# The first weight unit of four layers on the scaled but not yet normalized activations

## The chip, the cores and the metric

The program runs on one core of one Trainium2 chip. The metric is the device time of one execution in microseconds (us). The kernel before takes 989.41 us, the median of 3 runs (989.23 to 990.48).

## What is computed

Batch 1, 256 tokens, width 1024, all of it in fp32. Five residual layers follow each other: EVEN and ODD (the first block), then F1, MIX and F2 (the second block: FFN, mixer, FFN). Each opens with an RMS norm and a modulation whose shift and scale come from a conditioning vector, and closes with a gated residual update:

```python
def rms_norm(x, gain):
    y = x * lax.rsqrt(jnp.mean(x * x, axis=-1, keepdims=True) + EPS)
    return y * gain

def modulate(h, shift, scale):
    return h * (1 + scale[:, None, :]) + shift[:, None, :]
...
    h = modulate(rms_norm(x, ffn1_norm[l]), sh1, sc1)
    x = x + 0.5 * g1[:, None, :] * swiglu(h, ffn1_w_gate[l], ffn1_w_up[l], ffn1_w_down[l])
    h = modulate(rms_norm(x, mix_norm[l]), sh2, sc2)
    proj = h @ w_in[l]
...
def swiglu(h, w_gate, w_up, w_down):
    return (jax.nn.silu(h @ w_gate) * (h @ w_up)) @ w_down
```

Between ODD and F1 the first block's final norm is applied too, so two roots are needed there. Shifts, scales and gates are the columns of `cond @ W` with W of 1024 by 24576 in all; these weights are read like all the others.

## The kernel before

**Layout.** x and h are kept transposed: 8 tiles of 128 channels by 256 tokens. `xT` is the residual, `SQT` a work tile, `hh` and `hl` the high and low part of h (fp32 is split into two fp32r numbers, and a product is three matmuls: high by high, high by low, low by high). Weights come in units of 1 MB, each in two halves ("pieces") of 128x1024, from DRAM into `ring` (10 slots, filled in program order by SyncE), then ScalarE writes the high part into `WH` (4 slots, `cut`) and VectorE the low part into `WL` (4 slots, `cut`); both run two or three pieces ahead of TensorE, and a slot is free when TensorE has used its piece. `unit_list` writes the order of the units by hand, and `weave` strews the units of the modulation weights ("ada") between those of a layer; they are multiplied on VectorE (two instructions of 128x1024 per unit, L1676 or L1673), in `ada_places` behind the piece of the unit that follows.

**A unit.** `cols_T` is a unit of 256 output columns: for each of the 8 tiles of h 6 matmuls, 128 weight columns stationary and 256 tokens moving. `wide` (FFN gate and up, and others) has 128 tokens stationary and 512 weight columns moving. `out_rows` is a unit of the layer's output projection, which sums into `pacc` over all of a layer's units.

**Where two layers meet.** The last output unit (`finish`) gives `pacc` in four quarters of two tiles. VectorE adds each quarter to `xT` (`update`, L1770), ScalarE squares it (`squares`), TensorE sums the squares over the channels (64 small matmuls with ones, `stats`). VectorE takes the reciprocal root of two numbers per partition (`rsqrt`, 9 small instructions, L1710 to L1727), TensorE spreads it over the partitions (`spread`, bank `r`), and for each of the 8 tiles VectorE computes SQT = x times scale times root (L1756), ScalarE hh = SQT plus shift, VectorE hl = SQT plus shift minus hh (L1761). Only then does TensorE start on the first unit of the layer: `qk0` (ODD), `f1g0`, `wu0` (MIX), `f2g0`. Warm-up matmuls (`warm`) stand in the gap.

In the MIX layer `wu0` and `wu1` give the input of a state space part. ScalarE (12 copies per unit) and VectorE (4) rearrange it into `UR` (`urs`), and `s5_in(0)` and `s5_in(1)` on TensorE read it. `s5_in(0)` stands right behind `wu1`. In the FFN layers each block is a gate and an up unit and, one block later, a down unit; before it, the product is turned by four transposes (`turn`, L1022).

## Time and profile before

| | |
|---|---|
| median of 3 runs | 989.41 us |
| the profiled execution's own time | 992.07 us |
| its span in the trace | 990.3 us |
| PE busy | 954.0 us (96%) |
| weight loads busy | 876.7 us (89%) |
| VectorE (DVE) busy | 714.2 us (72%) |
| ScalarE (ACT) busy | 507.6 us (51%) |
| read from DRAM | 217.25 MB, 220 GB/s over the span |

The table is of the whole span. All queries and the hand-made schedules below are made on the one profiled execution, whose own time is 2.66 us above the median. A busy PE is not a PE at its peak, since matmuls overlap in the trace: work is told from waiting by the distance from one start to the next.

### The profile page before, as it was taken

To read this page: it belongs to the slowest core of one execution; us is meant where nothing else is said; L and a number is where in the kernel's file an instruction comes from. 1 tells how busy PE (TensorE), PEld (TensorE's weight loads), DVE (VectorE), ACT (ScalarE), POOL (GpSimd) and SP (SyncE) were. 2 spreads that over 40 slices of the span, in tenths; PEclk is the share of its full clock that TensorE was granted. 3 is DMA by queue.
4 is the path that set the end of the run, shared out by engine and by line. 5 is a ranking of instruction groups with operands and counts; after the bars stand their busy time and mean duration, and the time that the engine had idled before them with its cause. 6 is when DMAs were issued, how large, how long until landed. Compare 5 with 4: busy or idle time off the path is not lost.

```text
span 990.3 us, 17238 instructions
## 1 busy us (share of the span) xinstructions
PE 954.0 (96%) x7025; PEld 876.7 (89%) x7025; DVE 714.2 (72%) x994; ACT 507.6 (51%) x745; POOL 41.8 (4%) x68
## 2 busy tenths in 40 slices
PE   6999999999999999999999999999999999999998
PEld 6799999989799789999778888889998978898987
DVE  4778877767866766576899988977988765465554
ACT  4654364456544446544755456474646454444444
POOL 2100000000000003320100000000000000000000
PEclk9999999999999999999999999999999999999999
DMA  9987586844875894658378887776534457474731
GB/s 363 384 279 257 184 290 234 297 167 150 273 248 183 287 302 153 234 214 300 84 242 270 292 276 251 265 251 216 153 124 126 153 170 234 149 262 143 253 110 43
DMA packets 134247, 219.43 MB, mean 222 GB/s; under 512 B 8585, under 2 KB 100090, under 8 KB 134168
## 3 DMA queue, kind: packets, MB, share of 16 engines
q1 hardware_dynamic: 132416, 214.99, 64.9%
q0 software_dynamic: 992, 1.76, 0.7%
q10 hardware_dynamic: 760, 1.59, 0.4%
q8 instruction: 55, 0.90, 0.4%
q14 instruction: 24, 0.20, 0.1%
HBM read 217.25 MB, written 1.05 MB: 220 GB/s over the span
## 4 chain that ended last, share of the span: by engine, by line
PE 75%; DVE 11%; DMA 6%; issue 4%; ACT 4%; SPq 0%; ACTq 0%; DVEq 0%
PE pw L569 50%; PE pacc L569 24%; DMA ring<-in_odd_in_w 3%; DVE ACC L1676 3%; DVE WL L1660 2%; ACT WH L1175 1%; ACT AR L1175 1%; DMA ring<-in_ada_w 1%; DVE SQT L1756 1%; DVE hl L1761 1%; PE pw L1022 1%; DMA ring<-in_odd_out_w 1%; DMA ring<-in_ffn_w_down 1%; ACT hh L1175 1%; DMA cst<-in_consts 1%
## 5 line engine op out<-in xcount | busy, mean ns | idle before, releaser
L1175 ACT ACTIVATE WH<-ring 128x1024 fp32r<-128x1024 f32 x288 | 302.6, 1057 | 300.1 <-PE pw L569 125.0
L1660 DVE TENSOR_TENSOR WL<-ring,WH 128x1024 fp32r<-128x1024 f32 x288 | 348.0, 1224 | 90.8 <-ACT WH L1175 90.1
L569 PE MATMUL pacc<-YH,WH 128*128 128x256 f32 x672 | 192.9, 287 | 2.6 <-issue 1.7
L569 PE MATMUL pw<-hh,WH 128*128 128x256 f32 x704 | 187.8, 288 | 4.4 <-ACT AR L1175 2.1
L569 PE MATMUL pacc<-YH,WL 128*128 128x256 f32 x672 | 190.1, 283 | 0.0
L569 PE MATMUL pacc<-YL,WH 128*128 128x256 f32 x672 | 190.1, 283 | 0.0
L569 PE MATMUL pw<-hh,WL 128*128 128x256 f32 x704 | 184.9, 284 | 0.0
L569 PE MATMUL pw<-WH,hh 128*128 128x512 f32 x448 | 177.0, 395 | 4.4 <-DVE WL L1660 4.0
L569 PE MATMUL pw<-WL,hh 128*128 128x512 f32 x448 | 174.9, 390 | 0.0
L569 PEld LDWEIGHTS pw<-hh,WH 128*128 128x128 f32 x704 | 135.7, 193 | 9.2 <-issue 6.3
L569 PE MATMUL pw<-hl,WH 128*128 128x256 f32 x704 | 142.7, 284 | 0.0
L569 PE MATMUL pw<-WH,hl 128*128 128x512 f32 x448 | 138.1, 389 | 0.0
L569 PEld LDWEIGHTS pw<-hh,WL 128*128 128x128 f32 x704 | 135.8, 193 | 0.1
L569 PEld LDWEIGHTS pacc<-YH,WH 128*128 128x128 f32 x672 | 128.8, 192 | 5.9 <-issue 3.9
L569 PEld LDWEIGHTS pacc<-YL,WH 128*128 128x128 f32 x672 | 128.9, 192 | 0.7
L569 PEld LDWEIGHTS pacc<-YH,WL 128*128 128x128 f32 x672 | 128.8, 192 | 0.0
L1175 ACT ACTIVATE AR<-pw 128x512 f32<-128x512 f32 (+8 forms) x180 | 80.1, 466 | 94.3 <-PE pw L569 93.4
L1676 DVE SCALAR_TENSOR_TENSOR ACC<-ring,PC,ACC 128x1024 f32<-128x1024 f32 x95 | 121.7, 1281 | 2.9 <-DMA ring<-in_ada_w 2.7
L569 PEld LDWEIGHTS pw<-hl,WH 128*128 128x128 f32 x704 | 110.3, 193 | 0.1
L569 PEld LDWEIGHTS pw<-WH,hh 128*128 128x128 f32 x448 | 84.2, 188 | 25.1 <-DVE WL L1660 6.9
L569 PEld LDWEIGHTS pw<-WH,hl 128*128 128x128 f32 x448 | 84.1, 188 | 18.0
L569 PEld LDWEIGHTS pw<-WL,hh 128*128 128x128 f32 x448 | 84.2, 188 | 16.3
(272 smaller groups left out, 782.2 us busy)
## 6 DMA issues: line engine op xcount, KB each, us to landing
ring<-in_w_mod SPq DMA_DIRECT2D x72, 512.0 KB, 5.6
ring<-in_odd_in_w SPq DMA_DIRECT2D x56, 512.0 KB, 6.0
ring<-in_ada_w SPq DMA_DIRECT2D x48, 512.0 KB, 6.8
ring<-in_ffn_w_gate SPq DMA_DIRECT2D x88, 256.0 KB, 3.6
ring<-in_ffn_w_up SPq DMA_DIRECT2D x88, 256.0 KB, 4.5
ring<-in_ffn_w_down SPq DMA_DIRECT2D x44, 512.0 KB, 5.1
ring<-in_even_in_w SPq DMA_DIRECT2D x40, 512.0 KB, 7.4
ring<-in_even_out_w SPq DMA_DIRECT2D x16, 512.0 KB, 6.4
```

Of the source, the lines that this page charges most:

```text
L569: return eng.matmul(o, a, b, start=start, stop=stop, skip_group_check=True)
L1022: last = eng.transpose(pb[:, n * T + m * P:n * T + m * P + P], fbuf(blk, m)[:, n * P:n * P + P], ident)
L1175: return eng.activation(dst, src, func, **kw)
L1660: tt(WL[:, i % NL, :], slot(half_of(i)), WH[:, i % NH, :].bitcast(F32), SUB).then_inc(s_lo, 1)
L1676: stt(out=acc, in0=slot(g), scalar=wc, in1=acc, op0=MUL, op1=ADD).then_inc(s_ada, 1)
L1756: stt(out=SQT[:, k, :], in0=xT[:, k, :], scalar=GS[:, k:k + 1], in1=rb, op0=MUL, op1=MUL).then_inc(s_u, 1)
L1761: stt(out=hl[:, q, :], in0=SQT[:, q, :], scalar=m[:, q:q + 1], in1=hh[:, q, :].bitcast(F32), op0=ADD, op1=SUB).then_inc(s_hl, 1)
```

## The change

**What it does.** For ODD, F1, MIX and F2 the first unit no longer waits for the root. The product W(x·scale·root + shift) is written as root·W(x·scale) + W·shift: the root depends on the token alone and the shift on the channel alone.

- ScalarE writes x·scale into hh as soon as a quarter of x is updated (`early`), VectorE the low part (`early_lows`). hh and hl are two columns wider and hold the shift there, so one matmul of 258 moving columns does both products (`first`).
- Half of the sums of squares come after the first two tiles of that unit, the spreading of the root after the fifth.
- The other units read the fully modulated h, as before. It is now made while the first unit runs; h takes the place of x·scale.
- When the first unit is read, VectorE multiplies it by the root (`unnormed`, after all of `modulate`), then ScalarE adds the shift's product as a bias: into GQ (ODD), within the Silu (F1, F2), or into a new tile UT (MIX), from which `urs` now copies.
- The first FFN block's gate and up units are of the `cols_T` kind (96 matmuls of 256 columns in place of 48 of 512), and its four transposes are gone.
- The ada units leave the last 5 and, but for EVEN, the first 3 units of each layer. 20 of them now stand in 28 of ODD's 36 units (33 before), 16 in 25 of F1's 33 (30 before). QUIET names units at which no modulation work is done.
- All `warm` at these four places are gone. A table load of ScalarE's moves ahead of the squares (ODD), another into the units before (F1). GpSimd's four loads for F1's side work are issued after unit oo1, not oo7. Side work in F1 starts four pieces later.

```diff
@@ unit_list @@
-    def weave(side, from_, clear=0):
+    def weave(side, from_, clear=0, lead=0):
...
-            while k < len(side) and (2 * k + 1) * (len(main) - clear) <= 2 * i * len(side):
+            while k < len(side) and (2 * k + 1) * (len(main) - clear - lead) <= 2 * (i - lead) * len(side):
...
     def ffn(tag, Wg, Wu, Wd):
         for b in range(12):
-            if b < 11:
+            if b == 0:
+                cols(f"{tag}g0", Wg, 0)
+                cols(f"{tag}u0", Wu, 0)
+            elif b < 11:
...
-    weave(ada(a0, 2, 3) + ada(a1, 0, 2), at, 3)
+    weave(ada(a0, 2, 3) + ada(a1, 0, 2), at, 5)
...
-    weave(ada(a1, 2, 3) + ada(a2, 0, 4), at, 3)
+    weave(ada(a1, 2, 3) + ada(a2, 0, 4), at, 5, 3)
...
-    weave(ada(a2, 4, 8), at, 3)
+    weave(ada(a2, 4, 8), at, 5, 3)
...
-    weave(ada(a2, 8, 9), at)
+    weave(ada(a2, 8, 9), at, 5, 3)
...
+FIRST = [None, "qk0", "f1g0", "wu0", "f2g0"]
+QUIET = ("eo7", "qk0", "qk1", "oo7", "f1g0", "f1u0", "f1d10", "wu0", "wu1", "wo3", "f2g0", "f2u0", "f2d10")
@@ build @@
-        hh = sb("hh", [P, 8, T], F32R)
-        hl = sb("hl", [P, 8, T], F32R)
+        hh = sb("hh", [P, 8, T + 2], F32R)
+        hl = sb("hl", [P, 8, T + 2], F32R)
...
         def urs(copy, j, quadrants):
-            pb = v3(pw[place[f"wu{j}"]][:, :], 2).rearrange("p m (c s) -> p m c s", s=4)
+            src = UT if j == 0 else v3(pw[place["wu1"]][:, :], 2)
+            pb = src.rearrange("p m (c s) -> p m c s", s=4)
@@ TensorE @@
-            def norm_mod(L, z):
-                ada("tail " + TAIL[L - 1])
-                back(f"fin{L - 1}")
-                if L >= L_MIX:
-                    warm(5, f"warm{L}a")
-                spread(f"r{L}", 0, z, (s_u, 8 * L + 8), True)
-                warm(4, f"warm{L}b")
+            def first(L, z, c=0):
+                name = FIRST[L]
+                k, a = unit(name)
+                names = early_names(L)
+                bks = [open_(nm, None, True) for nm in names]
+                for half in range(2):
+                    H, Lo = piece(2 * k + half, a)
+                    for kk in range(4):
+                        i = 4 * half + kk
+                        if i == 2:
+                            later[L - 1]()
+                            back(f"fin{L - 1}")
+                        if i == 5:
+                            spread(f"r{L}", c, z, (s_rb, L), True)
+                        p.wait_ge(s_eh, 8 * (L - 1) + i + 1)
+                        for m, pb in enumerate(bks):
+                            mm(pb[:, 0:T + 2], H[:, kk, m * P:m * P + P], hh[:, i, :], i == 0, False)
+                            mm(pb[:, 0:T + 2], Lo[:, kk, m * P:m * P + P], hh[:, i, :], False, False)
+                        p.wait_ge(s_el, 8 * (L - 1) + i + 1)
+                        for m, pb in enumerate(bks):
+                            last = mm(pb[:, 0:T + 2], H[:, kk, m * P:m * P + P], hl[:, i, :], False, i == 7)
+                    last.then_inc(s_use, 1)
...
-            for j in range(2):
-                cols_T(L_MIX, f"wu{j}", [(s_ura, j + 1), (s_urd, j + 1)])
+            first(L_MIX, 5)
+            cols_T(L_MIX, "wu1", [(s_ura, 2), (s_urd, 2)])
             s5_in(0)
@@ ScalarE @@
+            def early(L, sh, c):
+                s.wait_ge(s_gs, L + 1)
+                s.wait_ge(*gone[f"ada{c}"])
+                s.wait_ge(*used(LAST_H[L]))
+                act(hh[:, :, T:T + 2], shift_cols(sh)).then_inc(s_esh, 1)
+                for q in range(4):
+                    ns = (2 * q, 2 * q + 1)
+                    if q == 3:
+                        cut_on(L - 1)
+                        squares(L - 1, ns)
+                    for n in ns:
+                        s.wait_ge(s_x, X_FIN[L - 1] + n + 1)
+                        act(hh[:, n, 0:T], xT[:, n, :], scale=GS[:, n:n + 1]).then_inc(s_eh, 1)
+                    if q < 3:
+                        squares(L - 1, ns)
+                k = unit(FIRST[L])
+                cut(2 * k)
+                modulate(L, sh, range(4))
+                cut(2 * k + 1)
+                modulate(L, sh, range(4, 8))
+                act(RB[L], pw[place[f"r{L}"]][:, 0:T]).then_inc(s_rb, 1)
+
+            def offsets(L, scale=1.0):
+                for m, nm in enumerate(early_names(L)):
+                    s.wait_ge(*full[nm])
+                    act(ES[:, m:m + 1], pw[place[nm]][:, T:T + 1], scale=scale).then_inc(s_es, 1)
...
-            for nm in ("wu0", "wu1", "wc0", "wv0"):
+            offsets(L_MIX)
+            for m, nm in enumerate(early_names(L_MIX)):
+                s.wait_ge(*gone[nm])
+                act(UT[:, m, :], UT[:, m, :], ACT.Identity, bias=ES[:, m:m + 1]).then_inc(s_ut, 1)
+            s.wait_ge(s_ut, 2)
+            urs(act, 0, (0, 1, 2)).then_inc(s_ura, 1)
+            for nm in ("wu1", "wc0", "wv0"):
                 win(nm)
@@ VectorE @@
+            def between(L, g, sh, root):
+                v.wait_ge(s_esh, L)
+                tt(hl[:, :, T:T + 2], shift_cols(sh), hh[:, :, T:T + 2].bitcast(F32), SUB)
+                update(L - 1, g, lambda q: early_lows(L, (2 * q - 2, 2 * q - 1)))
+                k = unit(FIRST[L])
+                cut(2 * k)
+                root()
+                early_lows(L, (6, 7))
+                mods[0] += 1
+                modulate(L, sh, range(4))
+                cut(2 * k + 1)
+                modulate(L, sh, range(4, 8))
+
+            def unnormed(L, dsts):
+                v.wait_ge(s_rb, L)
+                for m, nm in enumerate(early_names(L)):
+                    v.wait_ge(s_es, 2 * (L - 1) + m + 1)
+                    tt(dsts[m], RB[L], pw[place[nm]][:, 0:T], MUL).then_inc(s_bank[place[nm]], 1)
@@ GpSimd @@
-            g.wait_ge(*used("oo7"))
+            g.wait_ge(*used("oo1"))
```

**How instructions move.** On VectorE, where MIX hands over to F2 (`xT` is the update, `hl` the low part, `WL` a weight piece's low part, `RS` the root). Before, from the last weight pieces of MIX:

```order
L1660 TENSOR_TENSOR WL<-ring,WH 128x1024 x6
L1770 SCALAR_TENSOR_TENSOR xT<-pacc,MOD,xT 128x256 x8
L1745 SCALAR_TENSOR_TENSOR PC<-MOD,VC 128x8
L1710 TENSOR_SCALAR RS<-pw 128x2
L1720 TENSOR_SCALAR RS<-RS 128x2
```

Now:

```order
L1728 TENSOR_TENSOR WL<-ring,WH 128x1024 x6
L1813 SCALAR_TENSOR_TENSOR PC<-MOD,VC 128x8
L1845 TENSOR_TENSOR hl<-MOD,hh 128x8x2
L1868 SCALAR_TENSOR_TENSOR xT<-pacc,MOD,xT 128x256 x4
L1825 SCALAR_TENSOR_TENSOR hl<-xT,PC,hh 128x256 x2
L1868 SCALAR_TENSOR_TENSOR xT<-pacc,MOD,xT 128x256 x2
L1825 SCALAR_TENSOR_TENSOR hl<-xT,PC,hh 128x256 x2
L1868 SCALAR_TENSOR_TENSOR xT<-pacc,MOD,xT 128x256 x2
L1825 SCALAR_TENSOR_TENSOR hl<-xT,PC,hh 128x256 x2
L1728 TENSOR_TENSOR WL<-ring,WH 128x1024
L1778 TENSOR_SCALAR RS<-pw 128x2
L1788 TENSOR_SCALAR RS<-RS 128x2
```

The eight updates are taken apart by six of the low parts, and a weight piece stands ahead of the root.

The same engine at the end of this hand-over, from the last products x·scale·root (`SQT`) on. Before:

```order
L1756 SCALAR_TENSOR_TENSOR SQT<-xT,PC,pw 128x256
L1761 SCALAR_TENSOR_TENSOR hl<-SQT,MOD,hh 128x256
L1756 SCALAR_TENSOR_TENSOR SQT<-xT,PC,pw 128x256
L1761 SCALAR_TENSOR_TENSOR hl<-SQT,MOD,hh 128x256 x2
L1660 TENSOR_TENSOR WL<-ring,WH 128x1024 x4
L2192 TENSOR_TENSOR AR<-AR,pw 128x256 x2
```

Now:

```order
L1838 SCALAR_TENSOR_TENSOR hl<-SQT,MOD,hh 128x256
L1833 SCALAR_TENSOR_TENSOR SQT<-xT,PC,pw 128x256
L1838 SCALAR_TENSOR_TENSOR hl<-SQT,MOD,hh 128x256
L1833 SCALAR_TENSOR_TENSOR SQT<-xT,PC,pw 128x256
L1838 SCALAR_TENSOR_TENSOR hl<-SQT,MOD,hh 128x256 x2
L1860 TENSOR_TENSOR AR<-AR,pw 128x256 x2
L1728 TENSOR_TENSOR WL<-ring,WH 128x1024 x2
L2287 TENSOR_TENSOR AR<-AR,pw 128x256 x2
```

The first weight piece behind the hand-over stands behind two products more, `AR<-AR,pw`, which are the first unit times the root.

On ScalarE, where F1 hands over to MIX. Before, from the squares to the copies into UR of the first unit:

```order
L1175 ACTIVATE SQT<-xT 128x256 x8
L1175 ACTIVATE WH<-ring 128x1024
L1175 ACTIVATE hh<-SQT,MOD 128x256 x8
L1175 ACTIVATE WH<-ring 128x1024 x2
L1175 ACTIVATE AR<-pw 32x2x64 x12
```

Now, from the last two high parts of x·scale on:

```order
L1205 ACTIVATE hh<-xT,PC 128x256 x2
L1205 ACTIVATE WH<-ring 128x1024
L1205 ACTIVATE hh<-SQT,MOD 128x256 x4
L1205 ACTIVATE WH<-ring 128x1024
L1205 ACTIVATE hh<-SQT,MOD 128x256 x4
L1205 ACTIVATE AR<-pw 128x256
L1205 ACTIVATE RS<-pw 128x1 x2
L1205 ACTIVATE AR<-AR,RS 128x256 x2
L1205 ACTIVATE AR<-AR 32x2x64 x12
```

The 12 copies of `wu0` stood two pieces behind the eight high parts of h. They now stand behind a copy of the root's bank, two columns of the shift's product and two biases.

## Rows read from the trace of the kernel before

**Rows 1.** The page: busy time by engine, and the chain that ended last.
```profile
PE 954.0 (96%) x7025; PEld 876.7 (89%) x7025; DVE 714.2 (72%) x994; ACT 507.6 (51%) x745; POOL 41.8 (4%) x68
...
PE 75%; DVE 11%; DMA 6%; issue 4%; ACT 4%; SPq 0%; ACTq 0%; DVEq 0%
```

**Rows 2.** Timeline, PE, 784 to 809 us: start us, duration us, instruction, [idle before].
```profile
784.82 2.09 PE L569 MATMUL pw<-cst,SQT 128*64 128x64 f32 x64
...
788.78 0.68 PE L569 MATMUL pw<-cst,RS 128*128 128x128 f32 x4 [0.56 <-DVE RS L1727]
...
790.67 0.47 PE L569 MATMUL pw<-WH,hh 128*128 128x512 f32 x1 [0.31 <-ACT hh L1175]
...
797.63 0.50 PE L569 MATMUL pw<-WH,hh 128*128 128x512 f32 x1 [1.27 <-DVE WL L1660]
...
803.23 0.39 PE L569 MATMUL pw<-WH,hh 128*128 128x512 f32 x1
...
808.67 0.60 PE L1022 MATMUL pw<-cst,AR 128*128 128x128 f32 x4
```

**Rows 3.** Timeline, DVE, 781 to 801 us.
```profile
781.48 1.65 DVE L1770 SCALAR_TENSOR_TENSOR xT<-pacc,MOD,xT 128x256 f32<-128x256 f32 x4
...
787.03 0.16 DVE L1710 TENSOR_SCALAR RS<-pw 128x2 f32<-128x2 f32 x1 [1.02 <-PE pw L569]
...
789.50 0.87 DVE L1756 SCALAR_TENSOR_TENSOR SQT<-xT,PC,pw 128x256 f32<-128x256 f32 x2 [0.87 <-PE pw L569]
...
795.96 0.48 DVE L1761 SCALAR_TENSOR_TENSOR hl<-SQT,MOD,hh 128x256 fp32r<-128x256 f32 x1 [0.18 <-ACT hh L1175]
...
796.36 4.63 DVE L1660 TENSOR_TENSOR WL<-ring,WH 128x1024 fp32r<-128x1024 f32 x4
```

**Rows 4.** Timeline, ACT, 781 to 788 us.
```profile
781.99 1.59 ACT L1175 ACTIVATE SQT<-xT 128x256 f32<-128x256 f32 x4 [1.76 <-DVE xT L1770]
...
786.16 1.04 ACT L1175 ACTIVATE WH<-ring 128x1024 fp32r<-128x1024 f32 x1
```

**Rows 5.** Timeline, PE, the places to which the other three layers are followed.
```profile
222.65 0.28 PE L569 MATMUL pw<-hh,GRH 128*16 128x256 f32 x1
...
231.22 1.13 PE L569 MATMUL pw<-AR 16*128 16x256 f32 x8
...
492.79 0.39 PE L569 MATMUL pw<-WH,hh 128*128 128x512 f32 x1
...
701.35 3.68 PE L569 MATMUL pw<-AR 128*128 128x64 f32 x32
```

**Rows 6.** Timeline, DVE, last instruction ahead of each of these layers' updates.
```profile
205.21 1.22 DVE L1660 TENSOR_TENSOR WL<-ring,WH 128x1024 fp32r<-128x1024 f32 x1 [1.66 <-ACT WH L1175]
...
467.28 1.23 DVE L1660 TENSOR_TENSOR WL<-ring,WH 128x1024 fp32r<-128x1024 f32 x1 [1.65 <-ACT WH L1175]
...
678.44 0.17 DVE L2200 TENSOR_SCALAR PC<-MOD 128x8 f32<-128x8 f32 x1
```

**Rows 7.** Timeline, ACT, a table load and the copies to UR.
```profile
220.89 1.28 ACT L1316 ACT_TABLE_LOAD   x1
...
695.46 3.32 ACT L1175 ACTIVATE AR<-pw 32x128 f32<-32x128 f32 x12
```

**Rows 8.** Stretches: us, busy us of engines (instructions), PEclk, DMA share, GB/s.
```profile
210.00:214.00 4.00, 2.13 (x65) 2.02 (x62) 2.12 (x12) 1.75 (x3) 0.00 (x0) 1.00 0.02 6
...
214.00:218.00 4.00, 3.76 (x23) 3.50 (x22) 3.36 (x9) 1.92 (x4) 0.00 (x0) 0.62 0.01 4
...
320.00:326.00 6.00, 3.86 (x35) 2.91 (x34) 5.84 (x11) 1.64 (x3) 0.00 (x0) 1.00 0.95 334
```

**Rows 9.** A stretch of the F1 layer, columns as in rows 8.
```profile
490.00:670.00 180.00, 177.97 (x1097) 154.57 (x1096) 158.89 (x206) 102.07 (x152) 0.23 (x2) 1.00 0.78 259
```

**Rows 10.** Timeline, DVE and PE, 258 us: a half of a modulation unit, and a stall.
```profile
258.72 1.28 DVE L1676 SCALAR_TENSOR_TENSOR ACC<-ring,PC,ACC 128x1024 f32<-128x1024 f32 x1
...
258.85 0.50 PE L569 MATMUL pw<-WH,hh 128*128 128x512 f32 x1 [0.40 <-DVE WL L1660]
```

More of the change, by code:

```diff
@@ L223, in ada_places @@
                 held += [m - 2, m - 1]
-        else:
+        elif nm not in quiet:
             add(nm)
@@ L2182, in ffn @@
             def ffn(tag, y0, n0):
-                for blk in range(12):
+                pieces(f"{tag}u0")
+                if tag == "f1":
+                    side.rate = 1
+                b = place[f"{tag}u0"]
+                for m in range(2):
+                    v.wait_ge(*full[f"{tag}u0"])
+                    v.wait_ge(s_sl, n0 + m + 1)
+                    a = tt(fbuf(0, m), fbuf(0, m), pw[b][:, m * T:m * T + T], MUL)
+                a.then_inc(s_bank[b], 1)
+                for blk in range(1, 12):
                     if blk < 11:
@@ L2336, in _, with first_rows @@
             side.rate = 4
-            win("wu0")
-            win("wu1")
+            def first_rows():
+                v.wait_ge(s_ut, 2)
+                urs(copy, 0, (3,)).then_inc(s_urd, 1)
+            pieces("wu1", first_rows)
+            v.wait_ge(*full["wu1"])
+            urs(copy, 1, (3,)).then_inc(s_urd, 1)
             side.gens.append(s5_states(0))
```

232 lines of the change are left out of this document (120 added, 112 removed).

## The prediction

> **What bounds the kernel.** I read the page first. TensorE (PE) is busy for 96% of the span and holds 75% of the chain that ended last; VectorE (DVE) is next with 11% [rows 1]. So only time in which PE waits can be won, and of PE's own work the change removes next to none. Then I went through the timelines of the four places where a layer hands over to the next, MIX to F2 in full. PE has its last sums of squares from 784.82 to 786.9, spreads the root at 788.78, starts the first unit at 790.67 and waits once more at 797.63 for a weight piece's low part; the second FFN block starts at 803.23 [rows 2]. The last product starts 0.1 ahead of the sums, so 18.5 us pass until then for 13.0 us of work (2.1 of sums and 10.9 of the unit pair, 48 matmuls by 0.227, which is 5.44 for 24 from 803.23 to 808.67). 5.5 us are lost. The other three places lose about as much, so some 22 us of 990 lie here: the most that the change could aim at.
>
> What holds PE there is VectorE. From the root on it takes 0.395 us per instruction of 256 columns, two for each tile: 6.94 us from the first product (789.50) to the next weight piece (796.36, with 0.08 of overlap taken back) [rows 3]. PE needs 0.72 per tile (6 matmuls by 0.121). The question is what becomes of VectorE's chain when PE's wait goes.
>
> **VectorE's chain after the change, with MIX to F2 as the model.** I call x0 the start of the first update. A weight piece was at 780.34 to 781.57 and x0 at 781.48 [rows 3] (0.1 of overlap). Now the scale's columns, ScalarE's copy of the shift and its low part come first, three small instructions handed between engines, 0.2 each as in the root's steps: x0 = 782.15. From there:
>
> - Updates, squares and high parts. ScalarE now has four instructions per pair of tiles where it had two. Four take 1.59 [rows 4], the same as VectorE's two updates and two low parts. Three pairs need 0.5 + 3 x 1.6 = 5.3, then ScalarE puts a weight piece (1.04 [rows 4]) ahead of the last squares. VectorE's own piece waits for it and starts at x0 + 6.45.
> - That piece: 1.16 until the next instruction (4 in 4.63 [rows 3]): 7.6. The root: 1.75 from 787.03 to 788.78, the handing over to PE in it [rows 2, 3], 1.65 without: 9.3. Two low parts: 10.15.
> - The eight tiles of modulation: 6.94, plus the piece between their halves (1.16), plus 0.55, since high part and low part start anew: 18.8.
> - The two products of the first unit by the root: 0.8, then the next weight piece, 1.2: 20.85 in all.
>
> So the second block can start at 782.15 + 20.85 = 803.0, against 803.23. PE keeps up: from 784.7 on it has 2.1 of sums, 5.8 of the first unit and 0.5 of the spread, and it waits 1.1 for ScalarE (the last squares end at x0 + 7.1, 789.25; PE would be there at 788.1): the first unit ends at 794.3; the second unit ends 0.25 behind the last low part, at 801.2. There it waits again. The wait moved from ahead of the first unit to behind the second. The four transposes that go give 0.35 more [rows 2]. **F2: 0.6 us won.**
>
> **F1.** The last piece ahead is at 467.28 [rows 6], so it ends at 468.5. One small instruction more makes x0 = 469.4, four roots in place of two add 0.25: 490.5 against 492.79 [rows 5], and 0.35 from the transposes. **2.65 won.** It is more than in F2, since from x0 to the old mark are 23.4 us here and 21.1 there.
>
> **ODD.** The piece at 205.21 [rows 6] ends at 206.4, ScalarE's table load (1.28 [rows 7]) fits beside it: x0 = 207.15. The last low part ends at 226.0. The next matmuls, those with GRH, need a bank that the first product frees at 226.5, and take 2.75 (from 222.65 to 231.22 it was these and a unit of 5.8 [rows 5]). Two units and they end at 229.3; before at 231.1. **1.85 won.** The table load cost nothing where it was; here it has 0.1 us to spare.
>
> **MIX.** HG is at 678.44 [rows 6], x0 = 679.35, the last low part ends at 698.15. Both products are done at 699.05, the biases at 699.65. Then come the 12 copies into UR, 3.32 [rows 7], which lay under `wu1` before: 703.0. `s5_in(0)` stands right behind `wu1` on PE and began at 701.35 [rows 5]. **1.65 lost.** Queued behind it are `wc0` and all of the layer, and a PE that is 96% busy [rows 1] has little slack to take it up. PE stands still from 698.4 to 703.0, 4.6 us. After about 1.9 idle us in 210 to 214 the granted clock was 0.62 over the next 4 us, so 3 us at 1.2 GHz; in 320 to 326 2.1 idle us left it at 1.00 [rows 8]. Twice that should bring it down. It falls while PE still waits, so of the 1.5 us that 3 us at half clock can cost (bounds 0 and 1.5) I take 0.9. The Trainium skill ("TensorE: Matmul & The Clock Gate", section "Why this matters for your kernels") says the same: gaps between bursts of matmuls bring the lower clock back.
>
> The copies now read SBUF instead of PSUM; I priced them as before. The Trainium skill ("VectorE: DVE Perf Modes", section on the TRN2 errata) speaks against the change here: ScalarE pays 224 cycles per instruction from SBUF and 172 from PSUM. At 1.2 GHz that is an estimate of 0.04 us for each of 12, 0.5 us later; the sum would be a loss of 2.15 in place of 1.65. No row shows these copies from SBUF.
>
> **Edits at nothing.** 258 columns: a matmul of 256 takes 0.121 and one of 512 0.227, so 256 columns cost PE 0.114 at most and two more 0.001 each, 0.2 us over 192 matmuls, beside waits. 96 matmuls of 256 for 48 of 512: 11.6 for 10.9, hidden as long as VectorE sets the end; 0.7 twice if it doesn't. The warm-ups stood in the gap. GpSimd's early loads and the later side work of F1 meet no wait on PE.
>
> **Modulation units closer together.** In ODD six halves fall on `gv0` to `gv3` where four did, and there PE already waits for low parts (0.40 at 258.85, with a half of 1.28 just ahead [rows 10]); in F1 four halves leave the opening for a stretch in which VectorE is busy for 159 of 180 us [rows 9]. Bounds: nothing, or all six at 1.2, 7.2 us. A gain is possible too: the openings are free of halves, so VectorE may catch up. I take 0.6, near the low end, since VectorE has 21 idle us in F1.
>
> **Sum.** -1.85 - 2.65 - 0.6 + 1.65 + 0.9 + 0.6 = -1.95. On the profiled execution 992.07 becomes 990.1. It stands 2.66 above the median of 989.41; I take the difference over to the median: **987.5 us**. A measurement of this kernel tells about 0.2% (2 us) from no change, so below 987.4 is faster and above 991.4 slower. The forecast lies on that edge.
>
> **Rivals.**
> - *VectorE catches up* (0.25). The openings lose eight modulation halves, 4 in F1 and 4 in ODD before `gv0`, 1.2 us each of VectorE's time, 9.6 in all. If 0.4 of that stood in PE's way, as stalls like that of rows 10, 3.8 are won on top and the 0.6 isn't paid: 983.1. For it speaks that I let VectorE's backlog set three of four ends; against it, that the weights' ring is filled in order and a half held up holds the weights behind it.
> - *Modulation work becomes the bound* (0.2), the other side. Place: `gv0` to `gv3` and F1's middle. VectorE there has 2.3 us of pieces per unit, now 1.5 us of halves, and side work. It decides as soon as a weight piece's low part comes later than PE's 2.7 us per piece. Full price: the 6.6 us that I left out, 994.1; half of it 990.8; I expect 992 to 994.
> - *The hand-overs close* (0.05): VectorE's chain runs ahead and PE never waits. Four times 3.3 (790.67 less 786.9, less 0.5 for the spread): 976. Against it stands the chain above.
> - *The first unit doesn't start early*, as a wait of `early` or of a bank holds it. Then all four places get longer by 0.8 to 2 us; I count it with the slower case.
>
> **Chances.** Forecast 0.5: its own spread is 985.5 to 990, of which 0.2 is faster, 0.28 within 0.2% and 0.02 slower. Catching up gives 0.23 faster and 0.02 same; modulation 0.05 same and 0.15 slower; closing 0.05 faster. Together 0.48, 0.35, 0.17. The range for 8 in 10 leaves out the closing case and the upper half of the slower one: 983 to 991.8.
>
> **What would show it.** In the trace after: the first unit starting within 2 us of the last product, at all four places; two waits of PE for low parts, in the second unit and behind it, 1 to 2 us each in F1 and F2; `s5_in(0)` some 4.5 us behind `wu1` with a clock under 1.00 there; a VectorE chain of 18.8 from the first update to the last low part. If that chain is shorter by over 1 us, or PE waits for ScalarE's squares for over 2 us, the model is wrong. The number is wrong with right hand-overs if `gv0` to `gv3` or F1 change by over 2 us.

## The result, and the profile after

The changed kernel takes **1014.03 us** (median of 4 runs, 1012.67 to 1016.56), the kernel before 989.89 beside it: 1.0247 times as long, 95% interval 1.0225 to 1.027. Forecast were 987.5 in a range of 983.0 to 991.8. The profiled execution took 1014.64 us, its span is 1012.9.

The page of after, the lines that answer to [rows 1]:

```profile
PE 958.6 (95%) x7047; PEld 879.7 (87%) x7047; DVE 729.4 (72%) x1038; ACT 522.7 (52%) x796; POOL 42.8 (4%) x68
...
PE 69%; DVE 12%; DMA 8%; issue 5%; ACT 5%; SPq 0%; ACTq 0%; DVEq 0%
```

PE is busy for 4.6 us more, the span is 22.6 longer. PE's share of the chain falls from 75 to 69%. VectorE, DMA, ScalarE and "issue" gained it, so most of the time went into waits and not into work, and no single engine took it.

To see where, I put the start of every unit's last matmul of both kernels side by side. Each row gives the us between two of these marks (before e1 and e17, see the experiments):

| stretch | before | after | e1 | e17 |
|---|---|---|---|---|
| start to eo7 | 209.5 | 209.7 | 209.7 | 208.4 |
| eo7 to qk3 (hand-over to ODD) | 34.3 | 31.7 | 33.5 | 31.7 |
| qk3 to gv3 | 24.7 | 23.2 | 21.7 | 23.2 |
| og0 | 9.8 | **14.2** | 10.3 | 5.9 |
| og1 to og6 | 44.1 | 44.6 | 46.3 | 51.4 |
| og7 | 9.4 | **13.7** | 12.5 | 10.7 |
| sv0 to oo6 | 134.1 | 137.0 | 136.3 | 134.8 |
| oo6 to f1g2 (hand-over to F1) | 52.7 | 46.5 | 50.3 | 47.9 |
| f1g2 to f1d10 | 163.8 | **174.7** | 169.0 | 167.7 |
| f1d10 to wc0 (hand-over to MIX) | 28.2 | **37.2** | 28.2 | 28.1 |
| wc0 to wo3 | 74.1 | 73.7 | 74.0 | 73.6 |
| wo3 to f2u1 (hand-over to F2) | 29.8 | 28.9 | 29.7 | 28.9 |
| f2u1 to f2d10 | 166.7 | 168.5 | 166.7 | 168.5 |

Three hand-overs did become shorter, by 2.6, 6.2 and 0.9 us. The largest losses lie in four other places, in bold. Among neighbouring rows the place of a loss is not firm: e14 (see the experiments) differs from the kernel before by 128 unused bytes alone, and in its profiled execution og7 takes 13.8 and sv0 to oo6 130.8. Over og7 to oo6 together the two are 144.6 and 143.5, with 150.7 in after and 148.9 in e1; that sum is the safer reading.

**The hand-over to F2 goes as drawn up.** PE and VectorE there, as in [rows 2, 3]:

```profile
809.15 1.43 PE L585 MATMUL pw<-cst,SQT 128*64 128x64 f32 x32
812.77 0.61 PE L585 MATMUL pw<-cst,RS 128*128 128x128 f32 x4
819.42 0.36 PE L585 MATMUL pw<-hh,WH 128*128 128x256 f32 x1 [1.00 <-ACT hh L1205]
823.98 0.47 PE L585 MATMUL pw<-WH,hh 128*128 128x512 f32 x1 [1.33 <-DVE WL L1728]
```
```profile
803.64 1.66 DVE L1868 SCALAR_TENSOR_TENSOR xT<-pacc,MOD,xT 128x256 f32<-128x256 f32 x4
...
821.55 0.48 DVE L1838 SCALAR_TENSOR_TENSOR hl<-SQT,MOD,hh 128x256 fp32r<-128x256 f32 x1 [0.18 <-ACT hh L1205]
821.95 0.75 DVE L1860 TENSOR_TENSOR AR<-AR,pw 128x256 f32<-128x256 f32 x2
```

The reader is to see two waits of PE, 1.00 in the second unit and 1.33 behind it, and a VectorE chain of 18.3 us from the first update (803.64) to the products behind the last low part (821.95). The forecast had two waits for low parts of 1 to 2 us and a chain of 18.8; the first of the two ends with ScalarE's high part, not with a low part. F1 shows the same pair:

```profile
493.24 0.36 PE L585 MATMUL pw<-hh,WH 128*128 128x256 f32 x1 [1.02 <-ACT hh L1205]
497.81 0.47 PE L585 MATMUL pw<-WH,hh 128*128 128x512 f32 x1 [0.85 <-DVE WL L1728]
```

**og0 and og7.** PE, then ScalarE and VectorE ahead of the second wait:

```profile
268.14 2.20 PE L585 MATMUL pw<-AR 128*128 128x128 f32 x9 [3.18 <-DVE AR L2056]
```
```profile
328.76 1.08 PE L585 MATMUL pw<-ACC,cst 128*32 128x256 f32 x8 [4.52 <-DVE ACC L1744]
```
```profile
322.70 1.06 ACT L1205 ACTIVATE WH<-ring 128x1024 fp32r<-128x1024 f32 x1 [8.88 <-DMA ring<-in_odd_in_w]
```
```profile
323.86 1.23 DVE L1728 TENSOR_TENSOR WL<-ring,WH 128x1024 fp32r<-128x1024 f32 x1 [0.65 <-ACT WH L1205]
325.00 1.28 DVE L1744 SCALAR_TENSOR_TENSOR ACC<-ring,PC,ACC 128x1024 f32<-128x1024 f32 x1
326.20 1.22 DVE L1728 TENSOR_TENSOR WL<-ring,WH 128x1024 fp32r<-128x1024 f32 x1
327.33 1.28 DVE L1744 SCALAR_TENSOR_TENSOR ACC<-ring,PC,ACC 128x1024 f32<-128x1024 f32 x1
```

At 268 PE waits for the decay's last product, which the attention matrices (`at`) need. That product, before and after:

```profile
263.38 1.22 DVE L1957 TENSOR_TENSOR AR<-AR 128x1024 f32<-128x1024 f32 x1
```
```profile
266.87 1.22 DVE L2056 TENSOR_TENSOR AR<-AR 128x1024 f32<-128x1024 f32 x1
```

It starts 3.5 us later, while PE is through with gv3 3.9 us earlier (its last matmul at 264.6, before at 268.4). So og0 gives back a lead: at its end the changed kernel is 0.5 behind. At 328 PE waits for a modulation sum, the sum for halves that stand behind weight pieces, the pieces for a transfer that ScalarE had waited 8.88 us for.

**The hand-over to MIX.** ScalarE, PE, and stretches as in [rows 8]:

```profile
711.63 0.91 ACT L1205 ACTIVATE AR<-AR,RS 128x256 f32<-128x256 f32 x2 [0.85 <-DVE AR L1860]
712.57 5.22 ACT L1205 ACTIVATE AR<-AR 32x128 f32<-32x128 f32 x12
717.81 2.00 ACT L1205 ACTIVATE WH<-ring 128x1024 fp32r<-128x1024 f32 x2
719.72 3.31 ACT L1205 ACTIVATE AR<-pw 32x128 f32<-32x128 f32 x12
```
```profile
718.04 1.30 PE L585 MATMUL pw<-AR 128*128 128x64 f32 x5 [6.53 <-ACT AR L1205]
```
```profile
711.00:715.00 4.00, 0.51 (x5) 0.31 (x3) 3.02 (x8) 3.27 (x8) 0.00 (x0) 1.00 0.17 45
...
719.00:723.00 4.00, 4.00 (x21) 4.00 (x20) 3.87 (x7) 3.87 (x13) 0.00 (x0) 0.50 0.39 129
723.00:727.00 4.00, 4.00 (x20) 4.00 (x20) 2.88 (x5) 1.10 (x2) 0.00 (x0) 0.50 0.50 137
```

The 12 copies of `wu0`, now from SBUF, take 5.22 us; the 12 of `wu1` behind them, from PSUM, take 3.31, as in [rows 7]. PE waits 6.53 us for them, until 718.04. The granted clock falls to the lower level (0.50, 1.2 GHz) at 715.5, within the wait, and stays there until 729.2: PE runs the first 11.1 us behind the wait at half clock, though it is busy all the time. From the end of wu1 to the end of wc0 pass 21.2 us where it was 9.3: 6.5 of wait, and 5.4 more, which the half clock over those 11.1 us accounts for (5.6 at most). Ahead of it 2.9 us were won, so 9.0 are left.

**F1.** PE's waits of 1 us and more between f1g2 and f1d10:

```profile
530.91 0.77 PE L1062 MATMUL pw<-cst,AR 128*128 128x128 f32 x4 [1.10 <-DVE AR L2298]
...
587.32 0.77 PE L1062 MATMUL pw<-cst,AR 128*128 128x128 f32 x4 [1.84 <-DVE AR L2298]
...
593.90 0.64 PE L585 MATMUL pw<-ACC,cst 128*32 128x256 f32 x8 [2.54 <-issue]
...
689.57 0.39 PE L585 MATMUL pacc<-YH,WH 128*128 128x256 f32 x1 [1.85 <-DVE YL L1774]
```

In before this stretch shows one wait over 0.3, of 0.44. Some 1.6 of the 10.9 us are no waits: 17 units with 512 moving columns take 5.57 in place of 5.44, and 10 others 0.06 less each (e4, which has the wider rows alone, shows 1.4 for this stretch). What VectorE does ahead of the last of these waits:

```profile
685.96 2.83 DVE L2276 TENSOR_TENSOR AR<-AR 32x512 f32<-32x512 f32 x4
688.82 0.69 DVE L1774 TENSOR_TENSOR YL<-pw,YH 128x512 fp32r<-128x512 f32 x1
```

The four instructions of 0.7 us are the last step of F1's side work (`s5_skip`). Started four pieces later, it now ends just ahead of the low part `YL` that PE's next output unit needs; in e1 it is over at 672.6, 9.7 us ahead of `YL`.

### The profile page after: what moved, and what is told of

It is laid out like the page before. It is cut to its first block, busy times and chain, and to the rows that moved or that the text cites. A ratio compares the mean times of both kernels' runs of the same rounds, so it can differ in the third digit from the quotient of the medians.

```text
span 1012.9 us, 17393 instructions
## 1 busy us (share of the span) xinstructions
PE 958.6 (95%) x7047; PEld 879.7 (87%) x7047; DVE 729.4 (72%) x1038; ACT 522.7 (52%) x796; POOL 42.8 (4%) x68
## 4 chain that ended last, share of the span: by engine, by line
PE 69%; DVE 12%; DMA 8%; issue 5%; ACT 5%; SPq 0%; ACTq 0%; DVEq 0%
PE pw L585 46%; PE pacc L585 22%; DMA ring<-in_odd_in_w 4%; DVE ACC L1744 3%; DVE WL L1728 2%; ACT AR L1205 2%; ACT WH L1205 2%; DMA ring<-in_ffn_w_up 1%; DMA ring<-in_ada_w 1%; DVE SQT L1833 1%; DVE hl L1838 1%; DMA ring<-in_even_in_w 1%; ACT hh L1205 1%; PE pw L1062 1%; DMA cst<-in_consts 1%
## 5 line engine op out<-in xcount | busy, mean ns | idle before, releaser
L585 PE MATMUL pw<-hh,WH 128*128 128x256 f32 (+1 forms) x768 | 206.2, 290 | 4.1 <-ACT hh L1205 4.0
L585 PE MATMUL pw<-hh,WL 128*128 128x256 f32 (+1 forms) x768 | 201.8, 284 | 0.0
L585 PE MATMUL pw<-WH,hh 128*128 128x512 f32 x416 | 165.6, 398 | 2.6 <-DVE WL L1728 2.6
L585 PE MATMUL pw<-WL,hh 128*128 128x512 f32 x416 | 163.9, 394 | 0.0
L585 PEld LDWEIGHTS pw<-hh,WH 128*128 128x128 f32 x768 | 146.9, 191 | 10.1 <-issue 9.3
L585 PE MATMUL pw<-hl,WH 128*128 128x256 f32 (+1 forms) x768 | 155.2, 284 | 0.0
L585 PEld LDWEIGHTS pw<-hh,WL 128*128 128x128 f32 x768 | 147.3, 192 | 0.0
L585 PE MATMUL pw<-WH,hl 128*128 128x512 f32 x416 | 130.3, 394 | 0.0
L585 PEld LDWEIGHTS pw<-hl,WH 128*128 128x128 f32 x768 | 119.3, 191 | 0.1
L585 PEld LDWEIGHTS pw<-WH,hh 128*128 128x128 f32 x416 | 78.2, 188 | 23.0 <-issue 4.8
```

What stands on the lines that cost most here:

```text
L585: return eng.matmul(o, a, b, start=start, stop=stop, skip_group_check=True)
```

## The experiments

Theories at the start: **packing**, the denser weave of the modulation alone makes weights and sums late; against it **company**, that the later decay, F1's later side work and GpSimd's earlier loads do it. For MIX **copies and clock** against a chain behind it that is just as late. For the distance of matmuls the **wider rows** of hh and hl.

**e1: the new weave in the kernel before.**

```diff
-    weave(ada(a1, 2, 3) + ada(a2, 0, 4), at, 3)
+    weave(ada(a1, 2, 3) + ada(a2, 0, 4), at, 5, 3)
...
-    weave(ada(a2, 4, 8), at, 3)
+    weave(ada(a2, 4, 8), at, 5, 3)
```

`weave` takes its last parameter as in the change.

> The kernel before, with nothing changed but the places of the modulation units of ODD and F1: 20 of them in 28 units and 16 in 25, as in the change. Theory 'packing' (the denser weave alone makes weights and the sums of the modulation late in og0 to og7 and in the middle of F1): 8 to 14 us slower than before, with most of it between gv3 and sv0 and between f1g2 and f1d10, and ScalarE waiting longer for the ring's transfers there. Rival 'company' (the other edits of the change, the later start of the decay and of F1's side work, GpSimd's earlier loads, cost it): within 2 us of before.

998.49 us, 1.0094 (1.0064 to 1.0123): 8.4 us over the kernel before beside it (990.1), for other places of the same units. The column e1 has og7 3.2 and F1's middle 5.2 longer. Its PE there:

```profile
326.06 0.99 PE L569 MATMUL pw<-ACC,cst 128*32 128x256 f32 x8 [3.81 <-DVE ACC L1676]
...
565.93 0.77 PE L1022 MATMUL pw<-cst,AR 128*128 128x128 f32 x4 [1.79 <-DVE AR L2192]
...
591.51 0.64 PE L569 MATMUL pw<-ACC,cst 128*32 128x256 f32 x8 [2.07 <-issue]
```

The same kinds of wait as in after, but not the one at the end of F1. Packing holds for 8.4 of 24.1, and og0 (10.3) is not part of it.

**e2: the changed kernel, modulation from the layer's start on.**

```diff
-    weave(ada(a1, 2, 3) + ada(a2, 0, 4), at, 5, 3)
+    weave(ada(a1, 2, 3) + ada(a2, 0, 4), at, 5)
...
-    weave(ada(a2, 4, 8), at, 5, 3)
+    weave(ada(a2, 4, 8), at, 5)
...
-QUIET = ("eo7", "qk0", "qk1", "oo7", "f1g0", "f1u0", "f1d10", "wu0", "wu1", "wo3", "f2g0", "f2u0", "f2d10")
+QUIET = ("eo7", "qk0", "oo7", "f1g0", "f1d10", "wu0", "wu1", "wo3", "f2g0", "f2u0", "f2d10")
```

> The changed kernel with the modulation units of ODD and F1 starting at the layer's first unit again (20 in 31 units and 16 in 28; the last five stay free), and with halves allowed at qk1 and f1u0. Packing: 4 to 9 us faster than the changed kernel, the hand-overs at most 1.5 us longer each. Company: within 2 us of it.

1017.9 us, 1.0287 (1.0259 to 1.0315): 3.9 slower than the changed kernel. Less dense, and no better: neither theory's number came. The loss moved: og0 to og7 took 60.2 us in place of 72.4, but qk3 to gv3 34.0 in place of 23.2. gv3 took 12.5 us and f1g3 12.9, each with a wait of 4 to 4.6 ahead of a modulation sum that stood in the unit right behind its last half. So I formed "adjacent sums" (e7).

**e3: the mixer's input read later.**

```diff
             cols_T(L_MIX, "wu1", [(s_ura, 2), (s_urd, 2)])
+            cols_T(L_MIX, "wc0")
             s5_in(0)
-            cols_T(L_MIX, "wc0")
+            cols_T(L_MIX, "wv0")
             s5_in(1)
-            cols_T(L_MIX, "wv0")
...
-            urs(act, 0, (0, 1, 2)).then_inc(s_ura, 1)
...
+            pieces("wu1")
+            urs(act, 0, (0, 1)).then_inc(s_ura, 1)
+            s.wait_ge(*full["wu1"])
+            urs(act, 1, (0, 1, 2)).then_inc(s_ura, 1)
...
-                urs(copy, 0, (3,)).then_inc(s_urd, 1)
+                urs(copy, 0, (2, 3)).then_inc(s_urd, 1)
...
-            side.gens.append(s5_states(0))
             win("wc0")
-            side.gens.append(s5_states(1))
+            side.rate = 6
+            side.gens += [s5_states(0), s5_states(1)]
```

> The changed kernel with s5_in(0) behind wc0 and s5_in(1) behind wv0 on TensorE, ScalarE's weight pieces of wu1 ahead of the copies of wu0, and 8 of the 16 copies on VectorE where it had 4. Theory 'copies and clock' (11.9 us are lost from the end of wu1 to the end of wc0, as TensorE waits 6.5 us for 12 copies from SBUF and then runs at half clock): 7 to 11 us faster than the changed kernel, no clock under 0.9 in the mixer. Rival 'chain' (the state space part behind it is as late, and TensorE waits for it at wb0 or wc1 instead): at most 3 us faster, with a wait of 4 us or more in front of s5_out(0) or s5_turn(0).

1009.71 us, 1.0197 (1.0178 to 1.0215): 4.3 faster than the changed kernel, between the two. The clock stays at 1.00 in the mixer, and f1d10 to wc0 takes 24.4 in place of 37.2, wc0 to wo3 80.2 in place of 73.7. These two can't be read apart, since `s5_in(0)`, 3.7 us of work, now stands behind wc0: together they are 104.6 in place of 110.9, 6.3 less, with 102.3 before. F1's middle takes 2.2 more. In the mixer PE now waits for VectorE's state chain, whose first part the edit also starts later:

```profile
733.65 1.09 PE L585 MATMUL pw<-AR 128*64 128x128 f32 x16 [0.76 <-DVE AR L2399]
736.61 1.09 PE L585 MATMUL pw<-AR 128*64 128x128 f32 x16 [1.87 <-DVE AR L2404]
```

**e4: the kernel before with rows of 258.** `sb("hh", [P, 8, T])` and `hl` became `T + 2` wide, every use stays 256.

> The kernel before with hh and hl two columns wider (rows of 258, of which 256 are used) and nothing else. Theory 'row pitch' (the wider rows, or the addresses that they shift, change the distance of matmuls): units with 512 moving columns take 5.57 in place of 5.44 us and those with 256 moving columns 5.69 in place of 5.76, as in the changed kernel, and the sum over the kernel is within 2 us. Rival: nothing changes, both distances stay at 227 and 120 ns.

991.48 us, 1.0016 (1.0007 to 1.0026). The wide units take 5.57, the others 5.69, as expected; the sum is small, 1.6 us.

**e5: the changed kernel, the mixer as before.**

```diff
-            early(L_MIX, M2[:, 24:32], 9)
+            squares(L_F1)
+            cut_on(L_F1)
+            modulate(L_MIX, M2[:, 24:32])
```

and its like on PE (`first(L_MIX, 5)` out, spread and warm-ups in) and VectorE.

> The changed kernel with the mixer handed over as in the kernel before (root first, warm-ups, wu0 on the modulated h, its copies from PSUM); ODD, F1 and F2 stay as changed. Theory 'copies and clock': 8 to 10 us faster than the changed kernel (9.0 of the 22.4 us lie between the end of F1 and the end of wc0), no clock under 0.9 in the mixer. Rival 'the changed F1 hands its delay on': under 4 us faster.

1007.62 us, 1.0156 (1.0136 to 1.0177): 6.4 faster than the changed kernel. f1d10 to wc0 is 28.1, all 9 us are back; F1's middle took 3.0 more, with waits of 1.82 and 2.78 among those of the kinds shown above. Expected were 8 to 10 by one theory and under 4 by the other; neither came.

**e6: `at` behind og0.** On TensorE the unit og0 moved ahead of `p.wait_ge(s_kqe, 3)`, on ScalarE `gate(0)` ahead of the two evacuations.

> The changed kernel with the two attention matrices (at, 32 small matmuls on TensorE) behind the unit og0 in place of ahead of it, so that TensorE does not wait for the decay's last product. Theory 'late decay' (the matmuls with GRH and the decay behind them stand one unit later, since the first unit no longer has the modulated h): the 3.2 us of wait ahead of at and the half clock behind it are gone by og1, 3 to 4.5 us. At the kernel's end: the same, if og7's sum waits no longer for it. Rival 'ring' (TensorE is held in og6 to sv0 by weights and sums that come at their own time): og7 takes back what og0 gave, and the kernel is within 2 us of the changed one.

1013.57 us, 1.0222 (1.0202 to 1.0242). og0 took 7.6 in place of 14.2, og1 11.3 in place of 6.1: the wait moved on by a unit, and 1.4 us of it went. At f1g0 the kernel is 5.6 us ahead of the changed one (1.6 of which it had at eo7 already, before anything differed). At f1g6 2.7 are left, at the end 1.6, and in the median 0.5: F1's middle gave it back (178.9 for 174.7).

**e7: no sum right behind its halves.**

```diff
+            if summed and held and held[0] % 8 == 0:
+                continue
             for x in held:
                 half(nm, x)
```

> The changed kernel with one rule more for the places of the modulation work: the first halves of a new group of eight wait one unit if the group before was finished in the unit just ahead, so that a sum on TensorE (8 matmuls with ACC) never stands in the unit right behind its last half. It moves the sum of group 6 from og7 to sv0 and that of group 7 from sk0 to sq1, and nothing in F1. Theory 'adjacent sums' (the 4.5 us ahead of the sum in og7, the 0.5 in sk0 and the 4.55 and 4.0 us in gv3 and f1g3 of the run with the spread weave are all of this kind): 4 to 5.5 us less up to sv1, 3 to 5 us at the end. Rival 'ring': the weights of og7 and sv0 come as late as before (ScalarE waited 8.9 us for a transfer there), and under 1.5 us are won.

1023.98 us, 1.0334 (1.0318 to 1.0349): 10 us slower than the changed kernel, and the run that told most. At og7 it gained more than expected (7.3 in place of 13.65). Three units on, ScalarE and PE show this:

```profile
344.69 1.06 ACT L1207 ACTIVATE WH<-ring 128x1024 fp32r<-128x1024 f32 x1 [7.99 <-DMA ring<-in_odd_in_w]
```
```profile
348.99 0.77 PE L587 MATMUL pw<-WH,hh 128*128 128x512 f32 x1 [6.03 <-ACT AR L1207]
```

The halves that were held back by one unit kept their slots of the ring. SyncE's loads, and the first of the held halves on VectorE:

```profile
327.37 0.95 SPq L2577 DMA_DIRECT2D ring<-in_odd_in_w  x2
336.55 3.04 SPq L2577 DMA_DIRECT2D ring<-in_w_mod  x2
```
```profile
335.77 0.75 DVE L1743 TENSOR_SCALAR ACC<-ring,PC 128x1024 f32<-128x1024 f32 x1
```

SyncE issues nothing for 8.2 us and goes on when that half has ended (336.52). It fills the ring in program order, so the weights behind were loaded later, and sv2 took 13.2 us in place of 5.5. Here a half that is late costs more than one in the way.

**e8, e11, e12, e16, e17: repairs together.** All have the mixer of e5 and `at` of e6. e8 also has e7's rule, and the others do the column addition of group 9 already in oo7. For the rest they differ in where the modulation units stand: e8 and e11 in all but the last four units of ODD and F1, e12 from ODD's third and F1's second unit on, e16 as e11 but one unit later in ODD, e17 as e16 with two units moved by hand:

```diff
-    weave(ada(a1, 2, 3) + ada(a2, 0, 4), at, 5, 3)
+    weave(ada(a1, 2, 3) + ada(a2, 0, 4), at, 4, 0)
...
-    weave(ada(a2, 4, 8), at, 5, 3)
+    weave(ada(a2, 4, 8), at, 4, 0)
```

> All three repairs together with a wider weave: the mixer as before, at behind og0, the rule for the sums, and modulation units spread over all but the last four units of ODD and F1 (halves allowed at qk1 and f1u0). If the gains of the hand-overs of ODD, F1 and F2 (2.5, 3.7 and 0.9 us by the ends of units) stand and nothing else is left of the change's losses but the wider distance of matmuls: 983 to 990 us, so at or under the kernel before. If the ring and F1's side work hold TensorE anyway: 994 to 1000.

> Like e8 without the rule for the sums and with the modulation's column addition of group 9 ahead of the hand-over to F1 (in oo7) in place of behind it (f1u0), where it held a bank of f1g0. The 7.9 us that f1u0 lost in e8 (15.06 in place of 7.1) must be gone. If all else is as in e8, 991 to 993; if the sum of group 7 right behind its halves costs as little as in the changed kernel (0.5), the 5.7 us of wait in sk0 go too: 985 to 990.

> The mixer as before, at behind og0, and modulation units in ODD from the third unit on and in F1 from the second (20 in 29 and 16 in 27), without the rule for the sums. Sums right behind their halves: groups 5 and 8 in ODD, none in F1. Ring theory (it is the density that counts): between e11 and the changed kernel without its mixer part, 995 to 1003. If the pattern of sums counts more: under 995, with F1 from f1g2 to f1d10 in 165 us or less (163.8 before, 174.7 changed).

> e11 with ODD's modulation units starting one unit later (20 in 31). e11 waits 4.0 us for low parts in gv0 and gv1, with four halves and two more in the three units ahead. If that is the price of halves close behind the hand-over: 2 to 4 us faster than e11 at gv3, and at the end 988 to 991. If the sums of groups 5 and 8, now right behind their halves, take it back: 992 to 996.

> e16 with two of ODD's twenty modulation units moved by one unit of the layer, from og0 to og1 and from sk3 to oo0, so that the sums of groups 5 and 8 stand two units behind their last halves (og1, oo0) and not one (og0, sk3). If those two sums are what e16 lost there (og0 and og1 took 23.8 us in e16 and 16.1 in e11; sk3 and oo0 17.7 in e16), some 6 us of e16 go: 986 to 990, at or under the kernel before. If VectorE and the ring hold TensorE whatever the sums' places: 992 to 995, as e16.

| | us | against before (95%) | og0+og1 | sq0 | oo6 to f1g2 | f1g2 to f1d10 |
|---|---|---|---|---|---|---|
| e8 | 999.56 | 1.0088 (1.0073 to 1.0103) | 16.1 | 5.9 | 53.3 | 166.8 |
| e11 | 992.71 | 1.0039 (1.0026 to 1.0052) | 16.1 | 11.0 | 47.9 | 167.7 |
| e12 | 995.85 | 1.0067 (1.0045 to 1.0088) | 20.7 | 5.8 | 46.5 | 173.0 |
| e16 | 994.94 | 1.0048 (1.0031 to 1.0066) | 23.8 | 5.8 | 47.9 | 167.8 |
| e17 | 991.77 | 1.0017 (1.0004 to 1.003) | 19.6 | 5.8 | 47.9 | 167.7 |

e8 lost 7.9 us in f1u0, where an addition of a modulation column held a bank of `f1g0`; e11 has it back. e11 paid 5.1 in sq0 for the sum of group 7, but not the 6.4 that e8 had lost in sq1. e12 contradicts the rule by which I chose it: no sum in F1 stood right behind its last half there, and F1 took 173; its 995.85 lies where the ring theory had it. e16 won 3.9 in gv1 and 5.2 in sq0, and lost 7.7 in og0 and og1 and 4.4 in og7. e17 won back 4.2 in og0 and og1 and lost 1.5 between og7 and oo6 (oo0 is 2.4 longer): 3.2 in the medians where 6 were expected. It and e11, too close to rank, are the best versions with early first units, 21 to 22 us faster than the change and still no faster than before. In e17 the hand-overs of ODD, F1 and F2 are 8.3 us shorter than before (2.6, 4.8, 0.9), but qk3 to oo6 takes 4.0 more, F1's middle 3.9 and F2's 1.8: what the early units won is spent behind them. The wider rows account for some 1.6 in F1 and 1.8 in F2 (e4: 1.4 and 1.8); the rest was not taken apart.

**e9, e10, e13: what the weave is short of.** e9 and e10 are e1 with less VectorE work or smaller transfers, e13 is the kernel before with e9's cut. All three leave out most of the modulation's work or weights of ODD and F1.

```diff
-                            stt(out=acc, in0=slot(g), scalar=wc, in1=acc, op0=MUL, op1=ADD).then_inc(
+                            w = 64 if 40 <= m < 104 else 1024
+                            stt(out=acc[:, 0:w], in0=slot(g)[:, 0:w], scalar=wc, in1=acc[:, 0:w], op0=MUL, op1=ADD).then_inc(
```
```diff
+                        w = 128 if g // 2 in ada_units[20:52] else None
-                        eng.dma_start(v3(slot(g), k // 2), src[:, h * k // 2:(h + 1) * k // 2, :]).then_inc(
+                        eng.dma_start(v3(slot(g), k // 2)[:, :, 0:w], src[:, h * k // 2:(h + 1) * k // 2, 0:w]).then_inc(
```

> The kernel before with the new weave (as in e1), but seven of eight VectorE halves in ODD and F1 work on 64 of their 1024 columns: some 1.15 us less of VectorE per unit half, every transfer and every wait of the ring as in e1. Left out: most of the modulation of F1, MIX and F2. Theory 'VectorE' (the stalls of the denser weave come from halves in the way of low parts and sums): the 8.4 us that the weave costs are gone, at or under 990. Rival 'ring' (TensorE waits as weights land late, since more modulation weights are loaded between them): 995 or more, with ScalarE waiting for the ring's transfers in 240 to 480 as long as in e1 (68 us) or longer.

> The kernel before with the new weave (as in e1), but the modulation weights of ODD and F1 are loaded with 128 of their 1024 columns (64 KB in place of 512 KB), and VectorE works on the full width of the slot. Left out: most of the modulation's weights there. VectorE theory: 997 or more, since its work is the same. Ring theory: the 8.4 us of the weave are gone, 982 to 990, and ScalarE's waits for the ring in 240 to 480 fall under 15 us.

> The kernel before, its own weave, with the small halves of e9 (64 of 1024 columns for seven of eight halves in ODD and F1; most of that modulation is left out). If VectorE's halves are the whole price of the new weave, this run equals e9: 984 to 987. If the weave costs something by itself (ring, sums), it is 3 us or more faster than e9: 976 to 982.

985.74 us, 0.9957 (0.9943 to 0.9972); 986.57, 0.9973 (0.9962 to 0.9984); 982.26, 0.992 (0.9902 to 0.9938). Either cut takes 12 us off e1, more than the weave cost, so neither theory wins; that the two resources stand in one chain is how I read it. ScalarE's waits for the ring's pieces of `odd_in_w` (240 to 480 us; total, times, longest) in before, e1, e9, e10:

```profile
ACT WH L1175 <- DMA ring<-in_odd_in_w: 38.8, 11, 6.7
```
```profile
ACT WH L1175 <- DMA ring<-in_odd_in_w: 68.0, 22, 8.4
```
```profile
ACT WH L1175 <- DMA ring<-in_odd_in_w: 58.6, 21, 8.6
```
```profile
ACT WH L1175 <- DMA ring<-in_odd_in_w: 46.9, 17, 9.1
```

e9 waits for the ring nearly as long as e1 and is 12.8 us faster, as it should be if VectorE turns a late piece round at once. e10 did not fall under 15 us as the ring theory had it. With small halves in both, the new weave still costs 3.5 us (985.74 less 982.26); with full ones 8.4. By this comparison 3.5 are the order of the loads and sums, and the other 4.9 hang on the length of the halves. The small loads were not run in the kernel before, so e10's gain is not divided in this way.

**e14 and e15: width or address.** e14 is the kernel before with `gap = sb("gap", [P, 32])`, 128 bytes, ahead of YH. e15 is e11 with rows of 264.

> The kernel before with an unused tile of 128 bytes per partition between hl and YH: all later addresses are those of the changed kernel, the rows of hh and hl stay 256 wide. Theory 'row': 512-column units keep 5.44 us, 256-column units 5.76. Theory 'address': both change as in e4 (5.57 and 5.69). If only the 256-column units change (5.69) while the wide ones keep 5.44, the kernel gains 3 us or more: 984 to 988.

> e11 with rows of 264 in hh and hl (1056 bytes in place of 1032) and two small tiles shortened to make room. If the distance of 512-column matmuls depends on how the row's start lies (1032 bytes is a multiple of 8 only, 1056 of 32): 5.44 us per wide unit again, and 4 to 6 us faster than e11, 987 to 989. Rival: any width but 256 does it, and it equals e11.

989.13 us, 0.9989 (0.9978 to 1.0001), and 993.12, 1.0031 (1.0018 to 1.0044), as e11. The distance from one matmul's start to the next of its kind, ns, mean of the shorter nine tenths:

| | hh stationary, 512 moving | hh moving, 256 | YH moving, 256 |
|---|---|---|---|
| before (rows 256) | 227.1 | 119.7 | 119.8 |
| e14 (rows 256, YH 128 bytes on) | 227.1 | 119.7 | 118.5 |
| e4 (rows 258, YH 128 bytes on) | 231.7 | 118.4 | 118.5 |
| e15 (rows 264, YH 512 bytes on) | 232.1 | 117.4 | 119.7 |

The width of the row does the first two columns, the address of YH the third.

## Why the prediction was wrong, point by point

- **The hand-overs of ODD, F1 and F2** (forecast -1.85, -2.65, -0.6): right in mechanism, and in size for ODD and F2. Measured -2.6, -6.2 and -0.9. e1 alone shortens the first two openings by 0.8 and 2.5, since they are free of modulation; if that may be taken off, -1.8, -3.8 and -0.9 are left. It may not quite: e11, with modulation in both openings, still has -2.6 and -4.8. F1's term was too small either way. All four first units start within 1.7 us of the last product, as forecast.
- **"Modulation units closer together"** is the first step that failed. I took 0.6 out of 0 to 7.2; e1 measures 8.4 (6.3 to 12.2 by its interval), and that is net of the 3.3 that it wins in the two openings. I priced only the six halves in gv0 to gv3 and F1's start that changed places, and those stretches became shorter (qk3 to gv3 by 1.5 us). The price lay where the other units were packed to. The sentence that did not follow from its row was "I take 0.6, near the low end, since VectorE has 21 idle us in F1" [rows 9]: idle time of an engine in a chain with the ring says nothing of its slack. The rival "modulation work becomes the bound" had this mechanism, with 0.2 and too low a price. Of its two places F1's middle was right (5.2 in e1, 10.9 in all, over the 2 us that I had named as a sign); the other was not `gv0` to `gv3` but og1 to oo6.
- **MIX** (forecast +1.65 and +0.9): the mechanism was right, the sizes were not. `s5_in(0)` came 3.8 us later behind f1d10 than before, not 1.65. The copies took 5.22 and not 3.32, since I took the row of the PSUM copies [rows 7] for copies that read every fourth element from SBUF. PE's wait was 6.5 us and not 4.6. And the clock: I bounded its price by 3 us at half clock, from the one stretch of [rows 8]; PE worked 11.1 us at half clock, and that cost 5.4. Together +9.0 (f1d10 to wc0) in place of 2.55; in e5 6.4 of it reach the median. The Trainium skill ("TensorE: Matmul & The Clock Gate", section "Why this matters for your kernels") says that a gap between bursts brings the lower clock; the trace agrees (0.50 from 715.5 on, within the wait of 6.5).
- **og0, +4.4:** a step that the prediction does not have. It ended ODD's hand-over at the matmuls with GRH. What hangs on them, the decay, starts one unit later, and its last product ends at 268.1 where `at` could have begun at 265.0; before, it ended at 264.6 and `at` began behind gv3 at 268.4. Its absence is shown by e1 (og0 10.3) and by e6 (og0 and og1 together 18.9 for 20.3).
- **Edits at nothing:** "258 columns ... 0.2 us" looked at the added columns and not at the row. e4: 1.6 us (0.7 to 2.6). "GpSimd's early loads and the later side work of F1 meet no wait on PE" was wrong too, for the side work: the last step of it stands ahead of PE's wait of 1.85 at 689.57, which e3 and e12 have as well and before and e1 have not. F1's middle is 5.8 longer than in e1, some 1.6 of it by the rows and 1.85 by this wait; the other 2.3, in waits ahead of `turn` for VectorE's products, I did not take apart.
- **The sum** treated the terms as independent. e5 and e6 show that they aren't: 9.2 us won in MIX came out as 6.4, a lead of 5.6 at f1g0 as 0.5. F1's middle took 174.7, 176.9, 177.7, 178.9 and 175.7 us in the changed kernel, e3, e5, e6 and e7, which have the same modulation places in F1 and enter it up to 13 us apart.

## What to carry to other kernels

In a queue that is filled in order, a consumer's place in the program is a price for all that stands behind it: take a move of side work for a change of the whole schedule, and time it alone before anything is built on the opening that it leaves (here 8.4 us, where the three shorter hand-overs promised 5.1). Follow a moved product to its last reader, past the layer's hand-over, and take the price of a copy from a row with the same source memory and the same steps in it. Where a wait of PE is unavoidable, price the clock behind it too: here 6.5 us of wait were followed by 11.1 us at 1.2 GHz, which cost 5.4.
